# Two more units of gate logits as seven products ahead of attention, and attention's rows turned one step later

## The reference, cut to what matters

```
proj = u @ w_in                      # xp 512 | q 512 | k 512 | v 512 | gate_logits 2048
y_pool = pool_mixer(xp) @ w_branch_pool
z = q.k / 8                          # 8 heads of 64, strictly causal
a[t,s] = sigmoid(z[t,s]) * prod_{s<j<t} (1 - sigmoid(z[t,j]))
y_sb = (a @ v) @ w_branch_attn
g_pool, g_sb = split(sigmoid(gate_logits))
h = h + (g_pool * y_pool + g_sb * y_sb) @ w_out
```

## Time and profile before

| | |
|---|---|
| Median of 3 runs | 1917.36 us (1917.35 to 1918.03) |
| Profiled execution: its time | 1918.11 us |
| Profiled execution: its span, first to last instruction | 1916.2 us |
| TensorE busy | 1903.5 us (99%) |
| VectorE busy | 1372.2 us (72%) |
| ScalarE busy | 796.4 us (42%) |
| Granted TensorE clock | 0.999 |
| Seven-product units of the mixing block | 707.7 to 822 us |
| Attention, first filler to the end of the last | 909.3 to 1149.8 us |

### The profile page before, as it was taken

How to read it: one execution, slowest core, us unless ns; L and a number is a source line. 1 busy time by engine, 2 the same in 40 slices (tenths; PEclk the granted TensorE clock), 3 DMA queues, 4 the chain that set the end, 5 groups by cost and what they waited for, 6 DMA issues and landing times.

```text
span 1916.2 us, 24977 instructions
## 1 busy us (share of the span) xinstructions
PE 1903.5 (99%) x9010; PEld 1592.0 (83%) x9010; DVE 1372.2 (72%) x1677; ACT 796.4 (42%) x1175; POOL 115.9 (6%) x157
## 2 busy tenths in 40 slices
PE   9999999999999999999999999999999999999998
PEld 8888888888888888888888888898888888888887
DVE  6978777784566776488677768889777777756555
ACT  7423232323434544234676752474323232324344
POOL 1000000000000300000233220010000000000001
PEclk9999999999999999999999999999999999999999
DMA  5456654558676733416875447643545444677665
GB/s 165 144 198 230 223 181 140 199 189 306 208 240 201 195 110 132 132 50 181 226 174 148 128 139 260 197 138 119 178 144 196 149 169 153 216 264 244 206 192 206
DMA packets 258419, 348.24 MB, mean 182 GB/s; under 512 B 29344, under 2 KB 161184, under 8 KB 255008
## 3 DMA queue, kind: packets, MB, share of 16 engines
q1 hardware_dynamic: 258336, 347.15, 56.3%
HBM read 233.83 MB, written 112.99 MB: 181 GB/s over the span
## 4 chain that ended last, share of the span: by engine, by line
PE 97%; DVE 1%; DMA 1%; issue 0%; SPq 0%; ACT 0%; POOL 0%; POOLq 0%; DVEq 0%; ACTq 0%
PE bank L1263 40%; PE bank L1372 9%; PE bank L1319 9%; PE bank L1321 9%; PE bank L1320 9%; PE bank L1513 6%; PE bank L1215 3%; PE bank L1449 2%; PE bank L1421 2%; PE bank L1479 2%; PE bank L1585 2%; PE bank L1604 1%; PE bank L1190 1%; PE bank L1603 1%; PE bank L1570 1%; PE bank L1568 1%
## 5 line engine op out<-in xcount | busy, mean ns | idle before, releaser
L2253 DVE TENSOR_TENSOR dn_lo<-dn_lo_raw,dn_hi 128x1024 fp32r<-128x1024 f32 x149 | 181.9, 1224 | 149.6 <-ACT dn_hi L1788 149.1
L1263 PE MATMUL bank<-lo_t,wa_hi 128*128 128x512 f32 x656 | 252.8, 389 | 0.0
L1263 PE MATMUL bank<-hi_t,wa_hi 128*128 128x512 f32 x656 | 252.8, 389 | 0.0
L1263 PE MATMUL bank<-hi_t,wa_lo 128*128 128x512 f32 x656 | 252.8, 389 | 0.0
L1788 ACT ACTIVATE dn_hi<-dn_lo_raw 128x1024 fp32r<-128x1024 f32 x149 | 158.0, 1061 | 218.8 <-DMA dn_lo_raw<-act_dram 218.8
L1319 PE MATMUL bank<-dn_hi 128*128 128x512 f32 x596 | 232.7, 390 | 0.0
L1321 PE MATMUL bank<-dn_lo,dn_hi 128*128 128x512 f32 x596 | 231.9, 389 | 0.0
L1320 PE MATMUL bank<-dn_hi,dn_lo 128*128 128x512 f32 x596 | 231.9, 389 | 0.0
L1263 PE MATMUL bank<-hi_b,wa_hi 128*128 128x512 f32 x492 | 190.6, 389 | 1.0 <-DVE up L2387 1.0
L1263 PE MATMUL bank<-lo_b,wa_hi 128*128 128x512 f32 x492 | 190.5, 389 | 0.0
L1263 PE MATMUL bank<-hi_b,wa_lo 128*128 128x512 f32 x492 | 190.4, 389 | 0.0
(11 more groups left out here) (275 smaller groups left out, 3747.7 us busy)
## 6 DMA issues: line engine op xcount, KB each, us to landing
wa_lo_raw<-in_ffn_w_gate_up_dram SPq DMA_DIRECT2D x87, 512.0 KB, 5.0
dn_lo_raw<-act_dram SPq DMA_DIRECT2D x149, 256.0 KB, 4.2
act_dram<-g SPq DMA_DIRECT2D x44, 512.0 KB, 4.4
wd_t<-in_ffn_w_down_dram SPq DMA_DIRECT2D x44, 512.0 KB, 6.6
act_dram<-s_of SPq DMA_DIRECT2D x88, 256.0 KB, 6.5
wd_dram<-wd_t SPq DMA_DIRECT2D x22, 1024.0 KB, 6.0
dn_lo_raw<-wd_dram SPq DMA_DIRECT2D x85, 256.0 KB, 3.4
dn_lo_raw<-in_ffn_w_down_dram SPq DMA_DIRECT2D x64, 256.0 KB, 3.0
```

The lines of the kernel that those rows point to most:

```text
L1263: last = nc.tensor.matmul(acc, lhs, rhs, start=n == 0 and i != 2 and i < 5, stop=n == 11, skip_group_check=True)
L2253: return nc.vector.tensor_tensor(dst, raw, hi.bitcast(f32), ALU.subtract)
```

## The change

- `EARLY` goes from 4 to 8: `MIX_UNITS` gets two more seven-product units, so that all eight gate tiles of kind 1 are done ahead of attention. `GATE_UNITS` is then four units with two tiles of kind 0 each: 16 banks, 384 matmuls. Unit 0's weights are split ahead as before, those of the other three in attention. Every gate bank in attention now has the multiplication on GpSimd (16 of them, as before).
- With the same shares the first four steps get 10, 10, 6 and 5 filler matmuls, the others some 5, the four steps past the last tile that come ahead of the last one 3 each, and the last 36.
- `LAG = 3`: `turn`, `turned_hi` and `turned_lo` work on tile s - 3, `weigh` and what follows it come one step later (at odd steps), and the loop has one more step (`DRAIN` 5). On VectorE the low parts of tile s - 3 always come ahead of the scan of tile s - 1.
- The weights of a row get a fourth place (`a3`), and `betas(s)` waits for the transposes of tile s - 4.
- `gate_unit(1)` is issued behind `load_head(0)` in SyncE's queue, and its four pieces are split in steps 2, 5, 9 and 12 in place of 0, 1, 3 and 5.
- The ring's places follow from the number of tiles: `RING_AT` is (0, 2, 1) in place of (2, 1, 0).

```diff
--- before.py
+++ after.py
@@ -79,7 +79,7 @@
 V_FREE = {0: 3, 1: 3, 2: 4, 3: 4, 4: 6, 5: 6, 6: 6, 7: 6}
 
 
-EARLY = 4
+EARLY = 8
 GATE_UNITS = tuple(((0, j), (0, j + 1)) for j in range(0, EARLY, 2)) + tuple(((0, j), (1, j)) for j in range(EARLY, KT))
 NG = len(GATE_UNITS)
 
@@ -135,7 +135,8 @@
 
 
 CHUNKS = [sum(len(x["chunks"]) for x in TILES[:n]) for n in range(NA + 1)]
-DRAIN = 4
+DRAIN = 5
+LAG = 3
 V_DIFF, V_HIGH, V_LOW = ({NT + 3 + d: 1, 3 * NT + 3 + d: 2, 5 * NT + 3 + d: 3} for d in (0, 1, 5))
 POOL_AT = (0, 3, 2, 1)
 FIRST_LOW = next(n for n, x in enumerate(TILES) if x["qt"] < NT // 2)
@@ -183,7 +184,7 @@
 
 def piece_step(j, piece):
 
-    return gate_step(piece_start(j) + (7 + 18 * piece if j < NG - 1 else 1 + 6 * piece))
+    return gate_step(piece_start(j) + (20 if j == 1 else 7) + 18 * piece if j < NG - 1 else piece_start(j) + 1 + 6 * piece)
 
 
 BANKS_DONE = [[fb for fb in range(len(GATE_BANKS))
@@ -371,6 +372,7 @@
         keep = at("keep", [P, 2, SEQ], f32, X0 + 16384)
         a = at("a", [P, 2, SEQ], f32, X0 + 24576)
         a2 = at("a2", [P, SEQ], f32, o + 36864)
+        a3 = at("a3", [P, SEQ], f32, o + 16384)
         at_hi = at("at_hi", [P, NT, 2 * P], f32r, X0 + 32768)
         at_lo = at("at_lo", [P, NT, 2 * P], f32r, X0 + 40960)
 
@@ -1006,7 +1008,6 @@
 
             gate_unit(0)
             spill_pool_branch(2)
-            gate_unit(1)
 
             def load_pool_y(i):
 
@@ -1039,6 +1040,7 @@
                         sp_.dma_start(q_st[half, slot, c0:c1].bitcast(f32), qk_dram[part, pair, rows, c0:c1]).then_inc(quarter_in if hn == 0 and c0 == 0 else landed, 16)
 
             load_head(0)
+            gate_unit(1)
             spill_pool_branch(3)
             load_head(1)
             for b in range(4):
@@ -1104,12 +1106,12 @@
                 if s:
                     for fb in BANKS_DONE[s - 1]:
                         store_gate(fb)
-                    if s == NA:
+                    if s == NA + 1:
                         move_o(NA // 2 - 2, 3, slice(0, HALF // 2))
-                    elif s == NA + 2:
+                    elif s == NA + 3:
                         move_o(NA // 2 - 1, 4, slice(HALF // 2, HALF))
-                    elif s >= 4 and s % 2 == 0:
-                        store_o((s - 4) // 2)
+                    elif s >= LAG + 2 and s % 2:
+                        store_o((s - LAG - 2) // 2)
                     if s == O_STEP:
                         sp_.wait_ge(gate_ready, TH0_DONE + 1)
                         for b in range(2):
@@ -1171,7 +1173,7 @@
         @block.tensor
         def _(pe):
             def weights_of(n):
-                return a2[:, :] if n % 3 == 2 else a[:, n % 3, :]
+                return (a[:, 0, :], a[:, 1, :], a2[:, :], a3[:, :])[n % 4]
 
             def wait_bank(b, q):
 
@@ -1614,10 +1616,10 @@
                     continue
                 cut = g0 + (g1 - g0) // 2
                 gate_parts(g0, cut)
-                if s >= 4 and s % 2 == 0:
-                    weigh((s - 4) // 2)
-                if 2 <= s < NA + 2:
-                    turn(s - 2)
+                if s >= LAG + 2 and s % 2:
+                    weigh((s - LAG - 2) // 2)
+                if LAG <= s < NA + LAG:
+                    turn(s - LAG)
                 if s < NA:
                     n = len(TILES[s]["chunks"])
                     for part in range(n):
@@ -2151,8 +2153,8 @@
                     pool_stored()
                 if n >= 2:
                     act.wait_ge(a_ok, n - 1)
-                if n >= 3:
-                    act.wait_ge(t_ok, CHUNKS[n - 2])
+                if n >= 4:
+                    act.wait_ge(t_ok, CHUNKS[n - 3])
                 for part, (c0, c1) in enumerate(x_["chunks"]):
                     c = CHUNKS[n] + part
                     act.wait_ge(z_ok, c + 1)
@@ -2200,10 +2202,10 @@
                 nc.scalar.activation(gst[:, fb % 2, :], bank[:, 4 + fb % 2, :], ACT.Sigmoid).then_inc(gate_free[fb % 2], 1)
 
             for s in range(NA + DRAIN):
-                if s >= 4 and s % 2 == 0:
-                    take_o((s - 4) // 2)
-                if 2 <= s < NA + 2:
-                    turned_hi(s - 2)
+                if s >= LAG + 2 and s % 2:
+                    take_o((s - LAG - 2) // 2)
+                if LAG <= s < NA + LAG:
+                    turned_hi(s - LAG)
                 if s < NA:
                     betas(s)
                 if s in V_HIGH:
@@ -3051,13 +3053,10 @@
                     last.then_inc(wlo, 1)
 
             for s in range(NA + DRAIN):
-                turned_first = 2 <= s <= NA and TILES[s - 1]["qt"] in (1, 5, 3)
-                if turned_first:
-                    turned_lo(s - 2)
+                if LAG <= s < NA + LAG:
+                    turned_lo(s - LAG)
                 if 1 <= s <= NA:
                     weigh_keys(s - 1)
-                if 2 <= s < NA + 2 and not turned_first:
-                    turned_lo(s - 2)
                 for j, piece in PIECES_AT[s - 1] if s else ():
                     split_piece(j, piece)
                 if s in V_DIFF:
```

## The result

The changed kernel takes 1928.44 us (median of 4 runs, 1928.2 to 1929.43) against 1917.49 us before in the same comparison: ratio 1.0056, 95% interval [1.0043, 1.0069]. It is 11 us slower. The forecast was 1916.2 us, the range 1912.5 to 1922.5: a small gain was forecast, a loss came, outside the range. The profiled execution took 1928.49 us with a span of 1926.6 us.

A forecast was written before the change was run, and what follows sets the result against it. TensorE, busy 99% of the span, was taken as the bound. Terms -5.4 (matmuls) + 0.4 (start) + 1.8 (inside) + 2.0 (end) = -1.2 us gave 1916.9 us profiled, 1916.2 us as median; range 1912.5 to 1922.5.

The forecast's parts named there:

- The first term: Two units moved ahead of attention: net 24 matmuls fewer at 0.2266 us, -5.4 us, with TensorE never waiting in seven-product units.
- None of these is needed for several steps: Start of attention: gate unit 1's moved load delays second head and pooling rows by 1.1 us, at no cost.
- the keys' wait: Start of attention: TensorE's wait for keys becomes 2.0 us in place of 1.6, +0.4 us.
- The term for the inside of attention: Waits of TensorE within attention's heads grow from 0.7 to 2.5 us, +1.8 us; bounds 0 and 6 us.
- The steady wait named for the step of `qt` 0: In each of 8 heads `weigh` waits 0.25 us for VectorE's low parts and scan, 2.0 us in all.
- the "0.5 us" for pieces and differences: Inside attention: 0.5 us added for gate-weight pieces and differences of v falling on meetings with little to spare.
- The other meetings have 0.1 to 0.5 us to spare: Steady head in attention: apart from the `qt` 0 step, chains arrive 0.1 to 0.5 us before TensorE needs them.
- The term for the end: Past attention's last tile: waits of 0.6 and 0.8 us at `weigh`, 0.6 at the output, +2.0 us; bounds 0.6 and 3.
- Rival C: Attention output: its loads come late; if the first were 5 us late, +3.8 us, 1921.2 us; chance 0.06.
- The forecast wait ahead of the branch: Attention output, ahead of line 1449: TensorE waits 0.6 us for VectorE's chain, having 38 fillers in place of 40.
- Rival B: Attention: VectorE's fixed order, low parts ahead of the scan, becomes the bound; +6.6 us, 1924.0 us; chance 0.18.
- The rule on the masks: Attention: GpSimd masks and VectorE scans exclude each other on the shared port; by the rule some 1 us added.

The follow-up runs named there:

- Experiment 3: Changed kernel with pooling stores ahead of gate unit 1's load: 1930.48 us; also with split output loads, later pieces: 1927.07; only GpSimd products later: 1928.64; only load undone: 1925.58.
- all mends: Changed kernel with pieces and differences re-placed, second head ahead of gate unit 1's load, GpSimd's products later, output loads split, end loosened, VectorE's order kept: 1918.93 us.
- the edits: GpSimd's products and stores three steps later, output loads in two parts, first output sums inside the last steps; 4, 6, 8 tiles: 1915.82, 1915.87, 1918.93 us.
- experiment 2: Changed kernel with the attention output's loads in two parts, first three pieces at step 56, the last pair's two at step 59: 1926.65 us.

## Why the prediction was wrong

**The first term was right.** 24 matmuls fewer at 0.2266 us, and units of seven products with no wait: shown by the windows after.

**"None of these is needed for several steps" failed.** This sentence in the part on the start costed the place of gate unit 1's load at nothing. I forecast the keys' wait (0.4 us more, right: 2.1 us for 1.6), and listed the second head and the pooling rows behind the load, but not the pooling stores, and didn't ask which engine's next instruction needs them. The delay was mis-sized too: 1.1 us forecast, and the stores are issued until 955.6 in place of 952.1 with the load undone, 3.5 us. ScalarE's third pair of sigmoids needs the stores, ScalarE's pieces the load itself, GpSimd's first product, with masks behind it, the pooling rows. Undoing that place alone gives back 2.9 us with eight tiles (2.4 us of it read at the start); with six it is worth up to 9.7 us, together with the pieces' steps. Experiment 3 shows the mends beside it that gave nothing one by one.

**The term for the inside of attention, 1.8 us, was much too small.** The steady wait named for the step of `qt` 0 is there as sized: 0.1 to 0.4 us in each head from the second on (forecast 0.25). What was mis-sized is the "0.5 us" for pieces and differences: they cost 1.8, 0.6 and 0.8 us at three meetings, and 2.3 us by experiment (1921.26 against 1918.93). "The other meetings have 0.1 to 0.5 us to spare" was also wrong: turns in the first step of most heads, and once in the fifth, lose 0.2 to 0.4 us. In all, six heads grew by 6.8 us where 1.8 were forecast for all eight; 4.8 us of it are left in the best kernel with eight tiles, and its listed waits explain only a part of them. Which small gaps make up the rest, I can't show: ends of matmuls are modelled, and gaps of 0.1 us don't stand out.

**The term for the end, 2.0 us, was right where it was worked out and missed a queue.** The wait at the `weigh` before the last is 0.86 us (forecast 0.8). The last was forecast at 0.6 and is 2.8 us, plus the lower clock behind it. Rival C was near: it asked whether the output loads come late. They did not; they held up the store behind them. The forecast wait ahead of the branch (0.6 us) was not there, as I read it because TensorE itself had come later. With the loads split the last wait is 0.54 us, close to the 0.6 forecast, and the branch waits 0.4 us.

**Rival B had the right sign and over half of the size (6.6 us for 11) by luck.** Its mechanism, low parts ahead of the scan, isn't borne out: with thick filler the same order costs 1 to 2 us at most, later turn included, the other order costs 12 us more, and mends that leave the order alone take back 9.5 us. VectorE idles 53 us, more than B's 43, yet most of it is not the cause.

**The rule on the masks was right and cost nothing.** The 64 masks of GpSimd took 0.66 us on average before and 1.09 us after (median 0.43 and 1.13):

```profile
L3193 POOL TENSOR_SCALAR_AFFINE_SELECT a<-a x64: 293/1132/2180, 950.5 to 1140.4; 128x128 f32<-128x128 f32 x64
```

One that starts at 1029.03, beside a scan from 1028.84 to 1031.12, ends at 1031.21, 0.1 us behind the scan's end. But the mask's own scan stands behind that scan and the low parts anyway: VectorE waits only once for a mask, 2.7 us in the first head, and that mask stood behind GpSimd's wait for `pool_y`. So the 1 us that the rule was to add isn't seen.

**How it sums up.** The prediction's own terms give 201.2 us for attention (197.0 + 0.4 + 1.8 + 2.0; its "about 199" doesn't follow from them), and attention took 213.2. With all mends it is 9.5 us less by the medians, and the profiled execution shows where the rest stands: against the kernel before, less fillers, 1.4 us less at the start, 4.8 us more in the six heads and 3.3 us more at the end, together 6.7 us. The parts one by one (2.9 the load's place, 2.3 pieces and differences, 1.8 output loads, by differences of medians) don't simply add up, and what makes up the 6.7 us stays open. The saving is 5.4, so eight tiles end 1 us above the kernel before. With the edits (and with 8 tiles the pieces placed by hand too), 4, 6 and 8 tiles take 1915.8, 1915.9 and 1918.9 us, with own times of 79.8, 81.4 and 85.7 us: by these medians the first moved unit saves 2.7 us and pays 2.8, the second saves 2.7 and pays 5.7. That what thin filler costs grows faster than what seven products save fits this and isn't shown by it: each time has an interval of 1.7 us either way, and the three kernels differ in the place of the load and of the pieces too. The two best kernels stand 1.8 us under the kernel before, at the edge of what was measured; neither is shown to be faster.

## What to carry to other kernels

When a load is moved in an in-order queue, write down for each transfer that it passes which engine's next instruction waits for it, and what stands behind that instruction; "not needed yet" has to be shown for each. When filler is taken from a stage, small operations with no deadline of their own (pieces, differences, products of a side branch) become the ones that are late: their places have to be found again before the saving can be judged. A mend that gives nothing may be right and only not the last link, so mends of one place are tried together. And a mend is read first in the stretch that it touches, as the output loads show: 3.9 us there, 1.8 in the whole.

## What had not been expected of the hardware

A stop of TensorE can cost more than itself, and its length alone doesn't say whether it will. Windows from just ahead of the restart on, of other kernels here: first the one with all mends and six tiles but the late load (stop of 4.99 us), then the one with all mends and the load ahead (1.76 us), then the one with only pieces and differences put back (1.96 us). The last two stops are the same wait for keys, at the same place:

```profile
949.90:953.00 3.10, 3.04 (x13) 2.72 (x14) 3.08 (x6) 1.76 (x5) 0.59 (x2) 0.55 1.28 258
```

```profile
951.90:955.90 4.00, 3.94 (x11) 3.12 (x12) 2.04 (x1) 1.08 (x2) 0.00 (x0) 0.61 0.94 314
```

```profile
951.70:955.70 4.00, 3.93 (x18) 3.28 (x19) 2.04 (x1) 2.00 (x5) 0.02 (x1) 1.00 0.97 318
```

In the traces of all kernels here TensorE has 45 stops of 1.4 us or more in and around attention. Behind each of the 11 stops of 2.37 us and more the granted clock was at or near the lower level, 0.50 to 0.68 on average over the 4 us after the restart. Behind the 16 stops of 1.40 to 1.74 us it stayed at 1.00. Of the 18 between 1.76 and 2.22 us it fell behind ten and stayed behind eight, the longest of these (2.22 us) among the eight. By the window at 951.90 and the one of the end, a fall costs 1.6 to 1.7 us of work, by my estimate. So the stop of 2.8 us at the end cost about 4.5 us, and an execution in which a stop of some 2 us falls out well or badly can differ by 1.7 us with no edit at all, as the start in experiment 2 and the end in the kernel with the load undone show. That this is also what spreads the times of the unprofiled executions wasn't looked at.
